# First head's expert indices made alone and early, and two raw weight rooms instead of four for the last two query blocks

## The reference, cut to what matters

```python
q = (xt @ w_query).reshape(T, PEER_HEADS, PEER_KEY_DIM)
s1 = jnp.einsum('thd,hkd->thk', q[..., :PEER_HALF], sub_keys_1).astype(jnp.float32)
s2 = jnp.einsum('thd,hkd->thk', q[..., PEER_HALF:], sub_keys_2).astype(jnp.float32)
v1, i1 = lax.top_k(s1, PEER_TOPK)
v2, i2 = lax.top_k(s2, PEER_TOPK)
cand = (v1[..., :, None] + v2[..., None, :]).reshape(T, PEER_HEADS, PEER_TOPK * PEER_TOPK)
top_s, pos = lax.top_k(cand, PEER_TOPK)
eidx = jnp.take_along_axis(cand_idx, pos, axis=-1)
...
u = expert_down[ei]
a = jax.nn.gelu(jnp.einsum('cd,ced->ce', xi, u)).astype(jnp.float32)
w = (a * gi).astype(xi.dtype)
return jnp.einsum('ce,ced->cd', w, expert_up[ei])
```

## Time and profile before

| | us |
|---|---|
| median of 3 runs | 1952.4 |
| lowest, highest | 1950.53, 1957.28 |
| the profiled execution, device time | 1953.55 |
| its span | 1951.8 |
| granted TensorE clock, mean | 0.979 |

### The profile page before, as it was taken

One profiled execution on the slowest core, in us unless ns is written; L12 is line 12 of the kernel. 1 busy time (PEld: TensorE's weight loads), 2 busy tenths in 40 slices (PEclk: granted clock), 3 DMA queues, 4 the chain that ended last, 5 costly groups with the idle time before them and its releaser, 6 DMA issues.

```text
span 1951.8 us, 26465 instructions
## 1 busy us (share of the span) xinstructions
PE 1814.4 (93%) x10535; PEld 1500.8 (77%) x10535; DVE 1498.7 (77%) x2001; ACT 856.5 (44%) x1262; POOL 566.3 (29%) x369
## 2 busy tenths in 40 slices
PE   8999999999999989979989857679999999999997
PEld 7979987888899879968788744467767776777765
DVE  5354447444456556999999999999989999899888
ACT  4333336444433343323333289864344433344344
POOL 1302300000000000556567668842332113222221
PEclk9999999999999999989999989989999999999999
DMA  7864550355556644899999999989999999999996
GB/s 261 299 226 146 174 170 22 125 179 192 184 182 225 237 162 163 312 426 426 419 426 425 422 372 405 422 362 414 421 426 427 427 427 428 427 428 427 427 427 239
DMA packets 142677, 620.26 MB, mean 318 GB/s; under 512 B 9680, under 2 KB 20192, under 8 KB 84464
## 3 DMA queue, kind: packets, MB, share of 16 engines
q0 software_dynamic: 46352, 336.11, 41.5%
q1 hardware_dynamic: 93712, 280.05, 38.5%
q10 hardware_dynamic: 2512, 2.75, 0.4%
HBM read 616.77 MB, written 2.10 MB: 317 GB/s over the span
## 4 chain that ended last, share of the span: by engine, by line
PE 55%; DVE 23%; DMA 11%; issue 6%; ACT 3%; POOL 1%; SPq 0%; DVEq 0%; ACTq 0%
PE psum L679 54%; DVE down_rows L2306 11%; DMA u_raw<-in_peer_expert_up_dram 10%; POOL down_rows L1359 1%; DVE u_lo L2438 1%; DVE late_sum L2459 1%; ACT u_hi L1814 1%; DVE w_lo L1945 1%; DMA down_rows<-in_peer_expert_down_dram,eidx 1%; DMA x_in<-in_x_dram 0%; PE psum L697 0%; DVE late_rows L2306 0%; DVE onehot L2258 0%; DVE onehot L2261 0%; DVE key L2263 0%
## 5 line engine op out<-in xcount | busy, mean ns | idle before, releaser
L1945 DVE TENSOR_TENSOR w_lo<-raw,w_hi 128x2048 fp32r<-128x2048 f32 x124 | 286.1, 2307 | 337.6 <-ACT w_hi L1460 337.5
L1359 POOL DMA_INDIRECT down_rows<-in_peer_expert_down_dram,eidx x155 | 274.5, 1771 | 630.2 <-DVE eidx L2267 550.5
L1460 ACT CAST w_hi<-raw 128x2048 fp32r<-128x2048 f32 x124 | 236.6, 1908 | 397.4 <-PE psum L679 397.3
L679 PE MATMUL psum<-act_both,w_hi 128*128 128x256 f32 (+1 forms) x1664 | 390.1, 320 | 0.0
L1814 ACT CAST u_hi<-u_raw 128x2048 fp32r<-128x2048 f32 x112 | 214.3, 1913 | 359.7 <-DMA u_raw<-in_peer_expert_up_dram 354.3
L679 PE MATMUL psum<-act_both,w_lo 128*128 128x256 f32 x1088 | 307.0, 282 | 0.0
L679 PEld LDWEIGHTS psum<-act_both,w_hi 128*128 128x128 f32 x1664 | 276.1, 191 | 24.6 <-issue 0.6
L2438 DVE TENSOR_TENSOR u_lo<-u_raw,u_hi 128x2048 fp32r<-128x2048 f32 x112 | 256.5, 2290 | 0.0
L679 PEld LDWEIGHTS psum<-act_both,w_lo 128*128 128x128 f32 x1088 | 207.6, 191 | 0.0
L2306 DVE CUSTOM_DVE_ANT_0 down_rows<-down_rows,xn 128x2048 f32<-128x2048 f32 x91 | 205.4, 2288 | 0.6 <-DVE ind L2216 0.4
L679 PE MATMUL psum<-w_hi,act_both 128*128 128x512 f32 x640 | 201.5, 393 | 0.2 <-DVE w_lo L1945 0.2
(11 more groups left out here) (344 smaller groups left out, 3049.8 us busy)
## 6 DMA issues: line engine op xcount, KB each, us to landing
u_raw<-in_peer_expert_up_dram SPq DMA_DIRECT2D x128, 1024.0 KB, 11.9
raw<-in_w_in_dram SPq DMA_DIRECT2D x76, 1024.0 KB, 5.0
raw<-in_w_out_dram SPq DMA_DIRECT2D x16, 1024.0 KB, 5.0
raw<-in_peer_w_query_dram SPq DMA_DIRECT2D x16, 1024.0 KB, 5.0
raw<-in_w_up_nsa_dram SPq DMA_DIRECT2D x8, 1024.0 KB, 4.9
raw<-in_w_up_fox_dram SPq DMA_DIRECT2D x8, 1024.0 KB, 5.0
cmp_w<-in_k_cmp_w_dram SPq DMA_DIRECT2D x4, 1024.0 KB, 10.7
cmp_w<-in_v_cmp_w_dram SPq DMA_DIRECT2D x4, 1024.0 KB, 10.8
```

The costliest lines, as they stand in the source:

```text
L679: return nc.tensor.matmul(*a, skip_group_check=True, **k)
L1359: nc.gpsimd.indirect_dma_start(rows[:], None, table, bass.IndirectOffsetOnAxis(ap=eidx[:, half, slot:slot + 1], axis=0)).then_inc(landed, 16)
L1460: nc.scalar.copy(w_hi[:, p % 2], raw[:, p]).then_inc(hi_done, 1)
L1945: tt(w_lo[:, p % 2], raw[:, p], f32(w_hi[:, p % 2]), ALU.subtract).then_inc(lo_done, 1)
```

## The change

The diff, cut to what decides:

```diff
+RAW_PAIR = 29
-        def uses(b):
+        def index_sets(t):
+            return 1 if t < TOPK else t // (2 * TOPK) + 2
+        def raw_room(b, p):
+            return p % 2 if isinstance(b, int) and b >= RAW_PAIR else p
+        def uses(b, p):
+            if isinstance(b, int) and b >= RAW_PAIR:
+                return RAW_PAIR + 2 * (b - RAW_PAIR) + p // 2 + 1
             return b + 1
...
-        order = [8, 9, 10, 0, 8, 1, 9, 10, 4, 6, 2, 0, 3, 8, 1, 5, 7]
-        ring = [4, 6, 2, 0, 3, 1, 5, 7]
+        order = [8, 9, 10, 2, 3, 8, 9, 10, 4, 6, 0, 2, 1, 3, 8, 5, 7]
+        ring = [4, 6, 0, 2, 1, 3, 5, 7]
...
                     if not first:
-                        sp.wait_ge(lo_done, 4 * (b - 1) + p + 1)
-                    sp.dma_start(raw[:, p], src(p)).then_inc(raw_loaded[p], 16)
+                        two = isinstance(b, int) and 4 * b + p >= 4 * RAW_PAIR + 2
+                        sp.wait_ge(lo_done, 4 * b + p - (1 if two else 3))
+                    r = raw_room(b, p)
+                    sp.dma_start(raw[:, r], src(p)).then_inc(raw_loaded[r], 16)
...
+                elif r < 2:
+                    pool.wait_ge(lo_done, 4 * (NBLK - 1) + r + 3)
                 elif r < 4:
-                    pool.wait_ge(lo_done, 4 * (NBLK - 1) + r + 1)
+                    pool.wait_ge(lo_done, 4 * (RAW_PAIR - 1) + r + 1)
...
             top_lists(0, 0)
             lo_piece(QRY0 + 1, 3)
-            top_lists(0, 1)
+            top_sums(0, 0, 1)
 
             lo_piece(QRY0 + 2, 0)
-            top_sums(0, 0)
+            topk_end(0, 0, 1)
             evac(QRY0 + 1)
             lo_piece(QRY0 + 2, 1)
-            top_sums(0, 1)
+            top_lists(0, 1)
             lo_piece(QRY0 + 2, 2)
-            topk_end(0, 0, 2)
+            dot(0)
             lo_piece(QRY0 + 2, 3)
-            dve.wait_ge(ks_ps, 2)
-            top_lists(0, 2)
+            dot(1)
 
             lo_piece(NBLK - 1, 0)
-            top_lists(0, 3)
+            dot(2)
             evac(NBLK - 2)
             lo_piece(NBLK - 1, 1)
-            dot(0)
+            top_sums(0, 1, 2)
             lo_piece(NBLK - 1, 2)
-            dot(1)
-            dot(2)
+            topk_end(0, 1, 2)
             lo_piece(NBLK - 1, 3)
             dot(3)
             dot(4)
+            dve.wait_ge(ks_ps, 2)
+            top_lists(0, 2)
+            top_lists(0, 3)
             dot(5)
+            evac(NBLK - 1)
             dot(6)
-            evac(NBLK - 1)
             topk_weights(1, 0, 0, 2)
```

More of the change, by code:

```diff
@@ L650, in _ @@
             up_v = peer_expert_up[0].rearrange("(c p) d -> p c d", p=P)
-            sp.wait_ge(eidx_done, 8)
+            sp.wait_ge(eidx_done, index_sets(HALVES * SLOTS - 1))
             sp.wait_ge(down_used, SLOTS - len(PE_SLOTS))
@@ L1364, in _ @@
                 half, slot = t // SLOTS, t % SLOTS
-                if slot % (2 * TOPK) == 0:
-                    pool.wait_ge(eidx_done, t // (2 * TOPK) + 1)
+                if t in (0, TOPK) or t and slot % (2 * TOPK) == 0:
+                    pool.wait_ge(eidx_done, index_sets(t))
                 if t in PE_SLOTS:
@@ L1404, in late_gather @@
                        DENSE[1] + (j + PRE if dots_ else j - (LATE - PRE)), late_in[r])
-            pool.wait_ge(eidx_done, HALVES * PEER_H // 2)
+            pool.wait_ge(eidx_done, index_sets(HALVES * SLOTS - 1))
             for j in range(4):
@@ L1455, in hi_piece @@
             def hi_piece(b, p):
-                act.wait_ge(raw_loaded[p], uses(b) * 16)
+                r = raw_room(b, p)
+                act.wait_ge(raw_loaded[r], uses(b, p) * 16)
                 if not (isinstance(b, int) and b == 0 and p < 2):
                     act.wait_ge(piece_used, b * 4 + (p - 1))
-                nc.scalar.copy(w_hi[:, p % 2], raw[:, p]).then_inc(hi_done, 1)
+                nc.scalar.copy(w_hi[:, p % 2], raw[:, r]).then_inc(hi_done, 1)
             act.wait_ge(half_sum, 1)
@@ L1944, in lo_piece @@
                 dve.wait_ge(hi_done, b * 4 + (p + 1))
-                tt(w_lo[:, p % 2], raw[:, p], f32(w_hi[:, p % 2]), ALU.subtract).then_inc(lo_done, 1)
+                tt(w_lo[:, p % 2], raw[:, raw_room(b, p)], f32(w_hi[:, p % 2]), ALU.subtract).then_inc(lo_done, 1)
             def evac(b):
@@ L2226, in top_lists, with top_sums, top_sums_of @@
                     V.sem_inc(topk_read, 1)
-            def top_sums(half, h):
+            def top_sums(half, h0, h1):
+                for h in range(h0, h1):
+                    top_sums_of(half, h)
+            def top_sums_of(half, h):
                 cd = cand[:, h % 2]
@@ L2242, in topk_end @@
                 g = gw[half][:, hs]
-                tt(g, top[:, half, hs], top[:, half, hs, 0:1].to_broadcast([P, nh, TOPK]), ALU.subtract).then_inc(soft_in, 1)
+                ins = tt(g, top[:, half, hs], top[:, half, hs, 0:1].to_broadcast([P, nh, TOPK]), ALU.subtract)
+                if h1 % 2 == 0:
+                    ins.then_inc(soft_in, 1)
                 if half == 1 and h0 == 0:
@@ L2253, in topk_end @@
                 iota = const("iota").unsqueeze(1).to_broadcast([P, ns, TOPK])
-                eq = onehot[:]
+                eq = onehot[:, 0:nh]
                 oh = eq.rearrange("p h s c -> p (h s) c")
@@ L2547, in between @@
                     elif part == 1:
-                        top_sums(half, h)
-                        top_sums(half, h + 1)
+                        top_sums(half, h, h + 2)
                     else:
```

## The result

The changed kernel took 1977.24 us (median, 1971.55 to 1979.28) against 1952.4 us (1950.53 to 1957.28): a ratio of 1.012, 95% interval 1.0102 to 1.0138, or 24.8 us more. It is slower, as forecast, but by nearly twice the 12.8 us of the sum, and above the range. The profiled execution took 1978.04 us, 24.5 more than that of before (1953.55), so the two traces can account for all of it.

What follows compares the result with a forecast made beforehand. PE was taken to pace the last weight blocks and DVE, not DMA, the second stage. Lists +5.8 and two rooms +7.0 gave +12.8 us: 1966.4 us on the profiled execution, 1965.2 as median; range 1957 to 1970.

Steps and rivals of the forecast that it cites:

- the sum: Total forecast for the whole change: +5.8 us for the lists plus +7.0 us for the two rooms, +12.8 us.
- the mark: Moment (824.1 us before) when seven dots, lists of heads 0-3, indices of heads 0-1 and last evacuation are done; +12.8 us.
- still none: Sign expected in the new profile: DVE has no waits for gathers after the mark.
- Part 1, the lists: DVE's order behind the last lo: two heads' lists, 2.9 us each, now stand there too; +5.8 us on the mark.
- Part 2, early gathers: Head 0's index 13.3 us earlier, first gather landing near 786.7; DVE waits 2.8 us at dot(0); cost 0.
- Part 3, two rooms: Raw-piece loads issued later, beside gathers; (30, 0) lands near 799, PE stands 5.7 us; +7.0 us, bounds 0 and 10.8.
- The lead of 7.8 us: Time a raw-piece load was to have between its issue, two pieces before, and ACT wanting it.
- The turns by packet: Load and gather queues alternate packets, so a load of 2 KB runs beside 8 KB gathers gets a fifth: 12.3 us.
- The rival of light sharing: A load beside gathers gets half the bandwidth; two rooms cost 0 to 3 us, total +5.8 to +9; chance 0.21.
- absorbed: Lateness eaten where DVE waits anyway, at most 2.6 us; with light sharing +3 us, no change; chance 0.07.
- faster: DMA engines bound the second stage, so earlier gathers move the end by -5.5 us, at best -13.3; chance 0.06.
- rows 3: DVE's waits from 824 to 1290 us before: longest 1.7 us for PE, 0.4 for ACT, none for a gather.

Runs made afterwards that it cites:

- last rooms mended: Changed kernel with the tuple of rooms for the last gathers (from dot 142) set to (3, 7, 6, 0, 2, 1): 1966.67 us, ratio 1.0067.
- lists alone: Kernel before with the candidate lists of heads 2 and 3 made behind the last lo piece and dots 3 and 4: 1958.71 us, ratio 1.0023.
- four raw rooms: Changed kernel with the raw pieces back in rooms 0 to 3 and the old order of rooms, first three gathers still early: 1961.75 us, ratio 1.0052.
- two rooms alone: Kernel before with raw pieces from block 29 on in rooms 0 and 1 and gather rooms exchanged in all three lists: 1961.67 us, ratio 1.0042.
- ring alone: Kernel before with only the ring of rooms in the changed kernel's order, first and last rooms left as they were: 1965.55 us, ratio 1.0065.
- lists back: Changed kernel, last rooms mended, with the lists of heads 2 and 3 moved to between dot 0 and piece (29,3): 1963.46 us, ratio 1.0062.
- the last two kernels: Changed kernel with four raw rooms, old room order and lists ahead of (29,3) and (30,0): 1959.62 us; kernel before with DVE's steps one place earlier: 1952.73 us.
- the last kernel: Kernel before with DVE's steps of the last two query blocks each one place earlier: 1952.73 us against 1954.27, ratio 0.9995.

## Why the prediction was half right

**The step that failed** is a sentence in the first part: "Both kernels do the same from there on. What the mark moves, the end moves." The mark moved by what the sum could explain, but behind it the kernels don't do the same. The prediction counted the exchange of rooms as part of the move to two raw rooms and looked at it only where the first gathers are issued. It never followed the new ring to its seam with the last list. That one term, 10 us (the end moved 24.8 by the medians and 24.5 in the trace, the trace at the last dot ahead of the collision 14.8), is what carried the result out of the range: with the last rooms mended the kernel takes 1966.67 us, within it. No rival had it either. Two of the prediction's own signs do show it: DVE's waits for gathers behind the mark were to be "still none" and are 9.5 us, and the end of the second stage was to shift as much as the mark and shifted by 24.8 instead of 13.0.

**Part 1, the lists: right.** +5.8 forecast, 5.9 measured in four kernels (changed, last rooms mended, lists alone, four raw rooms), with nothing found again. That the index in two goes costs nothing also held where it stood ahead of the last lo.

**Part 2, early gathers: wrong in one row, and with a consequence.** The first gather came 15.4 us earlier (773.89 against 789.28, 13.3 forecast and 2.2 of a faster start). But the row that I took for its latency, 10.5 us, is not what an early gather takes. GpSimd's line of the changed kernel, its first gather:

```profile
DMA to landing us min/median/max: 5.7/5.7/5.7
```

So dot(0) did not wait (2.8 us forecast), and the rows began to move some 5 us sooner than in my sum. The Trainium skill's page "DMA: Bandwidth & Descriptors", section "Anatomy of one DMA — SWDGE (gpsimd) path", gives 4.4 us as an estimate, which is nearer to this row than the one I went by, and its consequence as the prediction put it, gathers that disturb the loads some 6 us sooner, is what happened. The 4.8 us that the first gather of the kernel before took more lie ahead of its data: its queue moved the first packets between 795 and 796 us, some 6 us behind the issue, and in the changed kernel between 775 and 776, some 1.5 us behind. Why isn't settled: its issue took 2.85 us on GpSimd instead of 1.07, and a load went out 2 us behind it.

**Part 3, two rooms: right in mechanism, wrong in which piece, 2.3 us short.** +7.0 forecast, +9.3 measured. (The lead of 7.8 us doesn't follow from the terms beside it, since 11.5 less 4.2 is 7.3; it is what the times used later give, 791.7 less 783.9, and nothing else hangs on it.) (29, 3), which I had 0.5 us late, was 8.0 late, since the gathers had begun sooner; (30, 0) was then 1.1 later still, and (30, 1) was in time. The loads' landing times in the changed kernel, those of (29, 3), of (30, 0), and of (30, 1) and (30, 2):

```profile
DMA to landing us min/median/max: 15.3/15.3/15.3
...
DMA to landing us min/median/max: 16.9/16.9/16.9
...
DMA to landing us min/median/max: 5.1/5.9/6.7
```

The 12 to 16 us that the prediction named for (30, 0) and (30, 1) came as 16.9 and 6.7. The turns by packet, which I had read from one tail of 1.5 us, now have a clean stretch. DMA queues (packets, MB, share) of the changed kernel from 784 to 786 us, while (29, 3) and (30, 0) move beside gathers:

```profile
q0 software_dynamic: 91, 0.68, 82.5%
q1 hardware_dynamic: 88, 0.18, 22.8%
```

and of the kernel before from 774 to 776, loads alone:

```profile
q1 hardware_dynamic: 378, 0.77, 99.5%
```

91 packets against 88, but 0.68 MB against 0.18: the loads get 90 GB/s instead of 385, not a fifth but 1 in 4.3. The kernel with two rooms alone shows 90 against 92 packets from 802 to 804. The rival of light sharing is out.

**Mark and end.** +12.8 was forecast for the mark, and the traces differ by 13.0 there. This agreement is partly luck: counted from (28, 3) it is 15.2, and the execution of the changed kernel came to that cast 2.2 us sooner. The rivals "absorbed" and "faster" are out: nothing was given back behind the mark, DVE never waited for a gather in the middle of the second stage before, as rows 3 said, and in the changed kernel DVE was as busy from 850 to 900 us with the DMA engines at 0.86.

## What to carry to other kernels

A list that hands out rooms is a schedule. Whoever renames entries in one such list has to look at every other list that names them, and at the seam of two lists count how many uses lie between one user of a room and the next; on a queue that issues in order, a distance of one stops everything behind it. A forecast that ends with "the same from there on" should be checked on the order of the queues down to the last instruction, not only where the edit stands. And where a load with short runs is to be hidden beside gathers with long rows, its lead has to be counted with the time that it takes beside them: here a lead of four pieces kept every load off the path (beside three early gathers), and a lead of two did not.

## What the runs showed of the hardware

- Two DMA queues shared packet for packet, not byte for byte: 91 to 88, and 90 to 92, in two kernels, with packets of 8 KB and 2 KB. A load of 1 MiB landed after 14.0 to 16.9 us where it moved beside gathers for most of its way, after 7.4 to 11.9 in the kernel with four raw rooms, where fewer gathers were in flight, and after 5.0 alone.
- The first gather of 1 MiB landed 5.7 us after its issue in the changed kernel, and 10.5 us in the kernel before.
- GpSimd's issue of a gather took from 0.94 us (behind a wait, in a row) to 3.0 us, for the same form of instruction. After the 15 us in which it stood idle, seven gathers went out in 10 us at 0.94 to 2.49 us each; what was short then was rows that had landed, not GpSimd's time.
- One wait of DVE for PE, ahead of the first `x_b` piece near 1162 to 1178 us, came in two main sizes: 1.7 us (before, last rooms mended, ring alone, lists alone, four raw rooms) and 3.4 us (two raw rooms alone, lists back, the last two kernels), with 2.8 in the changed kernel. It goes with PE's granted clock. In the 6 us ahead of the wait that clock is 1.00 in all five traces with 1.7 us, 0.66 or 0.67 in all four with 3.4, and 0.86 in the changed kernel, while in the 14 us ahead of these it is 1.00 and PE is busy 8.3 us in all ten. A clock of 1.00 is the level of 2.4 GHz; in the last kernel it stood at 0.50, the level of 1.2 GHz, from 1155.8 to 1161.8 us. The two stretches, in the kernel before and in the last one (columns as in the stretches above):

```profile
1155.60:1161.60 6.00, 4.01 (x22) 3.10 (x23) 6.00 (x6) 5.91 (x12) 3.80 (x2) 1.00 0.72 268
1161.60:1163.30 1.70, 1.63 (x11) 0.34 (x9) 0.05 (x2) 1.67 (x5) 1.40 (x2) 1.00 0.87 347
...
1153.80:1159.80 6.00, 4.95 (x21) 3.89 (x22) 5.99 (x6) 5.90 (x12) 3.86 (x2) 0.66 0.59 209
1159.80:1163.20 3.40, 3.40 (x14) 1.31 (x14) 0.03 (x1) 3.34 (x8) 1.73 (x2) 0.60 0.93 383
```

These 1.7 us are a part of the totals above that no edit was aimed at. Why the clock falls there in one kernel and not in the other isn't shown, nor whether another execution of the same kernel would do the same.
